# Conditioning products in column groups between the halves of the input projection, one stream of half-size weight units, gate rows by way of DRAM

## The reference

```python
mod = jnp.einsum('bd,de->be', jax.nn.silu(cvec), p['ada_w'][l]) + p['ada_b'][l]
sh1, sc1, g1, sh2, sc2, g2 = [m[:, None, :] for m in jnp.split(mod, 6, axis=-1)]
h = _rmsnorm(x, p['norm1_w'][l]) * (1 + sc1) + sh1
mix, s_fin = _mixer(h, rows, s0, l, p)      # input projection, 4 HGRN2 heads | Hyena long conv, output projection
x = x + g1 * mix
h = _rmsnorm(x, p['norm2_w'][l]) * (1 + sc2) + sh2
x = x + g2 * _convffn(h, rows, l, p)
```

## Time and profile before

| | |
|---|---|
| median of 3 runs | 1003.29 us (1003.22 to 1003.38) |
| span of the profiled execution, first to last instruction | 1001.4 us |
| PE busy | 979.4 us, 98% |
| DVE busy | 644.8 us, 64% |
| ACT busy | 346.6 us, 35% |
| DMA | 97.01 MB, mean 97 GB/s |

### The profile page before, as it was taken

How to read it: one execution, slowest core, us unless ns; L and a number is a source line. 1 busy time by engine, 2 the same in 40 slices (tenths; PEclk the granted TensorE clock), 3 DMA queues, 4 the chain that set the end, 5 groups by cost and what they waited for, 6 DMA issues and landing times.

```text
span 1001.4 us, 13700 instructions
## 1 busy us (share of the span) xinstructions
PE 979.4 (98%) x5628; PEld 835.9 (83%) x5628; DVE 644.8 (64%) x815; ACT 346.6 (35%) x590; POOL 0.2 (0%) x4
## 2 busy tenths in 40 slices
PE   7999999999999999999999999999999999999996
PEld 1257899999999994288849999988999988899985
DVE  4883458787786976947367656644566654466665
ACT  2552543444435313042164343311333331133333
POOL 0000000000000000000000000000000000000000
PEclk9999999999999999999999999999999999999999
DMA  7815332111211112824251212222122221121102
GB/s 288 329 72 173 122 126 85 49 43 44 80 52 44 48 48 98 294 81 154 99 210 43 85 47 80 85 84 85 43 85 84 84 85 68 59 85 63 45 20 105
DMA packets 17559, 97.01 MB, mean 97 GB/s; under 512 B 1912, under 2 KB 4472, under 8 KB 7257
## 3 DMA queue, kind: packets, MB, share of 16 engines
q1 hardware_dynamic: 17496, 96.14, 26.8%
HBM read 92.98 MB, written 3.15 MB: 96 GB/s over the span
## 4 chain that ended last, share of the span: by engine, by line
PE 93%; DVE 3%; ACT 2%; issue 1%; DMA 0%; SPq 0%; ACTq 0%; DVEq 0%
PE ps L1159 24%; PE ps L1161 24%; PE ps L1160 24%; PE ps L1178 7%; PE ps L1365 3%; PE ps L1484 1%; PE ps L1267 1%; PE ps L1377 1%; PE ps L1205 1%; PE ps L1297 1%; PE ps L1457 1%; PE ps L1258 1%; PE ps L1472 0%; PE ps L1385 0%; PE ps L1354 0%
## 5 line engine op out<-in xcount | busy, mean ns | idle before, releaser
L1159 PE MATMUL ps<-h_hi,w_hi 128*128 128x320 f32 x1152 | 360.8, 313 | 0.6 <-DVE h_lo L779 0.6
L1161 PE MATMUL ps<-h_hi,w_lo 128*128 128x320 f32 x1152 | 356.5, 309 | 0.0
L1160 PE MATMUL ps<-h_lo,w_hi 128*128 128x320 f32 x1152 | 356.3, 309 | 0.0
L771 DVE TENSOR_TENSOR w_lo<-raw,w_hi 128x1024 fp32r<-128x1024 f32 x114 | 138.8, 1225 | 140.8 <-ACT w_hi L487 135.9
L1159 PEld LDWEIGHTS ps<-h_hi,w_hi 128*128 128x128 f32 x1152 | 216.5, 188 | 1.6 <-DVE h_lo L779 0.9
L1160 PEld LDWEIGHTS ps<-h_lo,w_hi 128*128 128x128 f32 x1152 | 216.5, 188 | 0.3
L1161 PEld LDWEIGHTS ps<-h_hi,w_lo 128*128 128x128 f32 x1152 | 216.3, 188 | 0.0
L487 ACT ACTIVATE w_hi<-raw 128x1024 fp32r<-128x1024 f32 x114 | 118.7, 1051 | 134.4 <-PE ps L1161 128.1
L1159 PE MATMUL ps<-w_hi,a_hi 128*128 128x512 f32 x220 | 86.9, 395 | 0.0
L1160 PE MATMUL ps<-w_lo,a_hi 128*128 128x512 f32 x220 | 86.9, 395 | 0.0
L1161 PE MATMUL ps<-w_hi,a_lo 128*128 128x512 f32 x220 | 86.9, 395 | 0.0
(11 more groups left out here) (252 smaller groups left out, 1081.2 us busy)
## 6 DMA issues: line engine op xcount, KB each, us to landing
raw<-in_slots SPq DMA_DIRECT2D x76, 1024.0 KB, 4.8
xin<-in_x_sample SPq DMA_DIRECT2D x4, 512.0 KB, 6.9
x<-in_x_sample SPq DMA_DIRECT2D x4, 512.0 KB, 5.6
out_y_sample<-x SPq DMA_DIRECT2D x4, 512.0 KB, 2.6
decay<-in_decay SPq DMA_DIRECT2D x1, 1280.0 KB, 12.1
ktab<-in_ktab SPq DMA_DIRECT2D x1, 1024.0 KB, 6.8
utab<-in_utab SPq DMA_DIRECT2D x1, 1024.0 KB, 4.8
itab<-in_itab SPq DMA_DIRECT2D x1, 1024.0 KB, 4.9
```

The costliest lines, as they stand in the source:

```text
L771: V.tensor_tensor(w_lo[:, n % SPLITS, :], raw[:, s % RAWS, u * UNIT:(u + 1) * UNIT], w_hi[:, n % SPLITS, :].bitcast(F32), ALU.subtract).th ...
L1159: mm(out, lhs[0], rhs[0], start=first, stop=False)
L1160: mm(out, lhs[0], rhs[1], start=False, stop=False)
L1161: return mm(out, lhs[1], rhs[0], start=False, stop=last)
```

## The change

The 12 conditioning blocks are now all made alike: a quad (`ada_quad`) is four float32 products, each of one 128-row part of the sum, with a stationary side of 32 columns (silu(c) padded with zeros) and outputs on PSUM partitions 0, 32, 64 and 96, that is in four column groups. Two quads make a block. ACT copies all 128 partitions out, `ada_turn` transposes four 128 x 128 pieces, and DVE adds up the four groups (`sum_groups`). Blocks 0 to 3 stay at the start. The other eight stand in the input projection, at half products 7, 8 | 12, 13 | 19, 20 | 24, 25 | 31, 32 | 36, 37 | 43, 44 | 48, 49 (`ADA_QUAD`), with the turn behind the half product after (`ADA_TURN`: 9, 14, 21, ...). The blocks in stages 3 and 5, the fine units, and the gate products are gone: POOL writes the gate columns to a DRAM tensor `gates` and loads them back to all partitions. The stream of weights goes in units of 512 KB through a ring of five, with four split units and a lead of three. Half products use three PSUM banks where they used four; POOL issues the loads of masks, states, tables and x1 that SyncE issued. Within a head's tiles the last two (`g` and `hy`) are swapped, and the buffers `gs` and `cv` are single.

```diff
-RAWS = 3
-SPLITS = 3
+RING = 5
+SPLITS = 4
+def ada_half(e):
+    i = e - ADA_EARLY
+    return 7 + 12 * (i // 2) + 5 * (i % 2)
+ADA_QUAD = {ada_half(e) + j: (e, j) for e in range(ADA_EARLY, len(ADA_ORDER)) for j in range(2)}
+ADA_TURN = {ada_half(e) + 2: e for e in range(ADA_EARLY, len(ADA_ORDER))}
+ADA_SUM = {ada_half(e) + 3: e for e in range(ADA_EARLY, len(ADA_ORDER))}
+LEAD = 3
...
-            return n % 4 if n < NH else 5 + (n - NH) % 3
+            return n % 3 if n < NH else 5 + (n - NH) % 3
...
# POOL
+            def gate_out(which):
+                eng.wait_ge(sem("mod_ready"), ADA_ORDER.index(5 + 6 * which) + 1)
+                col = (2 + 3 * which) * KD
+                for s in range(2):
+                    eng.dma_start(gates[which, s].rearrange("(k p) -> p k", p=P), mod[:, col:col + KD, s],
+                                  allow_slow_non_contiguous=True).then_inc(sem("gate_out"), 16)
...
+            load(grow[:, :, :, :], gates.partition_broadcast(P), "ld_gates")
...
# ACT, loop over half products
                     spread(src, padm[:, i % 2, :], half, "half_free")
+                if n in ADA_TURN:
+                    ada_row(ADA_TURN[n])
                 if step_at(n):
                     step(*step_at(n))
...
-            for b in range(4, 8):
-                ada_row(b)
...
# PE
+            def ada_quad(e, j):
+                bank = ADA_BANK[e]
+                if j == 0 and e >= ADA_EARLY:
+                    eng.wait_ge(sem("ada_taken"), e)
+                elif j == 0 and bank in ADA_BANK[:e]:
+                    eng.wait_ge(sem("ada_row"), e - ADA_BANK[:e][::-1].index(bank))
+                for g in range(GROUPS):
+                    piece = arrived(eng, ("ada", e, 2 * j + g // 2))
+                    last = mm(ps[g * GROUP:(g + 1) * GROUP, bank, :], silu_c[:, GROUPS * j + g, :],
+                              piece[:, g % 2 * HW:(g % 2 + 1) * HW], start=(j == 0), stop=(j == 1))
+                last.then_inc(sem("ada_used"), 1)
+            def ada_turn(e):
+                eng.wait_ge(sem("ada_row"), e + 1)
+                if e:
+                    eng.wait_ge(sem("ada_taken"), e)
                 for k in range(4):
+                    last = nc.tensor.transpose(ps[:, TURN_BANK, k * P:(k + 1) * P],
+                                               ada_buffer(e)[:, k * P:(k + 1) * P], ident[:, :])
                 last.then_inc(sem("ada_cols"), 1)
...
-                half_product(n, tile_unit(n // 2), n % 2)
-                if n % 2 and n // 2 < MIXED - IV:
-                    fine_unit(IV + n // 2)
+                half_product(n, UNIT_TILE + n // 2, n % 2)
+                if n in ADA_QUAD:
+                    ada_quad(*ADA_QUAD[n])
+                if n in ADA_TURN:
+                    ada_turn(ADA_TURN[n])
                 if step_at(n):
                     step(*step_at(n))
...
-            eng.wait_ge(sem("uspec_ready"), 4)
-            ada_blocks(4, 8)
             eng.wait_ge(sem("zspec_ready"), 3)
...
-            ada_blocks(8, 10)
...
-            turn(xn, 1, (), gate_between)
-            eng.wait_ge(sem("row_ready"), 8)
+            turn(xn, 1, (), lambda k: None)
```

More of the change, by code:

```diff
@@ L101 @@
 ADA_SLOTS = [*range(ADA1), *range(SLOT_ADA2, SLOT_WOUT), *range(SLOT_ADA3, SLOT_FFN)]
-SLOT_UNITS = [RAW] * SLOT_FFN
+FFN_UNITS = []
+_s = SLOT_FFN
 for _f0, _nf in ROUNDS:
[L104 to L116, removed]
@@ L119, with weight_source @@
-UNIT_WOUT = MIXED + IV + len(TILES)
-UNIT_FFN = UNIT_WOUT + 2 * WOUT
+    _counts = [RAW] * _nf + 2 * [min(4, _nf - f) // 2 for f in range(0, _nf, 4)]
+    for _n in _counts:
+        FFN_UNITS += [(_s, _u) for _u in range(_n)]
+        _s += 1
+NSLOT = _s
+UNIT_TILE = IV
+UNIT_WOUT = IV + len(TILES)
+UNIT_FFN = UNIT_WOUT + 2 * WOUT
+NU = UNIT_FFN + len(FFN_UNITS)
+def weight_source(n):
+    if n < IV:
+        return SLOT_IV + n, 0
+    if n < UNIT_WOUT:
+        t = n - UNIT_TILE
+        at = t - (MIXED - IV)
+        return (SLOT_IV + IV + t, 0) if at < 0 else (SLOT_IV + MIXED + at // 2, at % 2)
+    if n < UNIT_FFN:
+        return SLOT_WOUT + (n - UNIT_WOUT) // 2, (n - UNIT_WOUT) % 2
+    return FFN_UNITS[n - UNIT_FFN]
@@ new lines, with stream @@
+ADA_SUM = {ada_half(e) + 3: e for e in range(ADA_EARLY, len(ADA_ORDER))}
+LEAD = 3
+def stream():
+    out = [("ada", e, q) for e in range(ADA_EARLY) for q in range(PIECES)]
+    out += [("weight", n) for n in range(UNIT_TILE + LEAD)]
+    for t in range(len(TILES)):
+        if t + LEAD < len(TILES):
+            out.append(("weight", UNIT_TILE + t + LEAD))
+        for n in (2 * t, 2 * t + 1):
+            if n in ADA_QUAD:
+                e, j = ADA_QUAD[n]
+                out += [("ada", e, 2 * j), ("ada", e, 2 * j + 1)]
+    return out + [("weight", n) for n in range(UNIT_WOUT, NU)]
@@ L579, in _ @@
                 take_odd(n)
-            for n in range(2, 2 * IV + 1):
+            for n in range(2, UNIT_TILE + LEAD):
                 split_hi(n)
@@ L617, in _ @@
                 src = ps[:, half_bank(n), 0:HT]
[L618 to L622 removed]
+                for unit in ahead(n):
+                    split_hi(unit)
                 eng.wait_ge(sem("half_made"), n + 1)
```

382 lines of the change are left out of this document (152 added, 230 removed).

## The result

The changed kernel takes 1029.43 us, median of 4 runs (1025.82 to 1030.04), against 1003.34 before: 1.0246 times as long, 95% interval 1.0227 to 1.0265. A second measurement on another chip gave 1.0238 (1.0221 to 1.0254). The forecast was 1035.7 us within 1014 to 1058, slower with 0.90. Direction and size came out. The profiled execution took 1025.82 us with a span of 1024.0. The terms are another matter: the quad was priced at more than twice what it costs, and two terms that cost more than forecast, the start and the gate products with norm2, made up for part of that. That the total came within 6.3 us is luck in part.

A forecast was written before the change was run, and what follows sets the result against it. TensorE was taken to bound the input projection, DVE to make the Hyena stage's hole. Terms 42.6 - 1.6 - 3.6 - 5.0 = +32.4 us on the 1001.4 span, 1033.8; with 1.9 for the median 1035.7 us, range 1014 to 1058.

The forecast's parts named there:

- start: Blocks 0 to 3 cost less TensorE time, but the second turn waits for a DVE sum: 0, bounds -3 and +3.
- input projection: Sixteen quads 36.0, turns 3.6, waits 10.4, fine units -7.4: +42.6 us, in the stage where TensorE sets the time.
- Hyena stage, to the output projection: Inverse transform can start 3.8 us earlier, less 2.2 charged for TensorE's start from idle: -1.6 us, bounds -3.8 and 0.
- gate products and norm2: Gate records in the output projection go, -3.6 us; norm2's first modulation comes earlier, less half the idle charge, -5.0 us.
- ConvFFN: Same products, and weight units of half the size arrive far ahead of use: 0 us.
- The mechanism: Conditioning moves out of two holes into the input projection, where TensorE has none; slower by over 0.2% given 0.90.
- The hidden work's end: Hyena stage: TensorE's four conditioning blocks fill a hole DVE makes anyway; only 3.8 us stick out and come back.
- Price of a quad: Input projection: eight passes of four matmuls take five pass times, 2.25 us a quad; bounds 0.87 and 3.5 us.
- rival 1: Input projection: the four column groups overlap fully, a quad takes 0.87 us; about +8 in all, 1012 us; chance 0.13.
- Turns and their waits: Input projection, eight times: four transposes at 0.45 us, and 1.3 us of TensorE waiting for ACT's copy; 3.6 and 10.4 us.
- Clock: Hyena stage: after idling 25.7 us TensorE's first products run slower, 2.2 us charged; half of it again at norm2.

The follow-up runs named there:

- e2: Changed kernel with blocks 6, 7, 10 and 11 run as quads in the Hyena stage, where PE waits for DVE's spectra: 1016.64 us, 1.0103.
- e6: Changed kernel with all four products of a quad written to the same 32 rows instead of four column groups: 1069.14 us, 1.0645.
- the second profile: The changed kernel itself measured once more, unedited, on another chip: 1028.42 us, 1.0238 of the kernel before.
- e4: Changed kernel with DVE's first two conditioning sums earlier and ScalarE's first two weight splits later, at the start only: 1026.65 us, 1.0216.
- e3: Changed kernel with the five x1 loads issued by SyncE inside the weight stream instead of by GpSimd: 1019.51 us, 1.016.
- e11: Changed kernel with later turns, four blocks in the Hyena stage, x1 on SyncE, reordered start, and unused products there and in the start's gaps: 1000.71 us, 0.9963.
- e9: Changed kernel with 30 unused products filling PE's empty stretch in the Hyena stage almost to its end: 1024.08 us, 1.0203.
- e7: Changed kernel with turns a half product later, four blocks in the Hyena stage, x1 on SyncE and the reordered start together: 1001.74 us, 0.9976.

## Why the prediction was right, step by step

The table's differences between before and after, against the sum on record:

| term | forecast | measured |
|---|---|---|
| start | 0 | +5.9 |
| input projection | +42.6 | +22.7 |
| Hyena stage, to the output projection | -1.6 | -1.3 |
| gate products and norm2 | -3.6 - 5.0 | -1.6 |
| ConvFFN | 0 | -3.1 |
| span | +32.4 | +22.6 |

Each length is from one profile of either kernel; how far a stage repeats is said above.

*The mechanism* held: conditioning moved out of two holes into the stage that PE sets, the holes stayed, and the time rose. The hidden work's end was right to 0.1 us: 3.8 forecast to come back in the Hyena stage, 49.89 - 46.13 = 3.76 measured. e2 shows the same from the other side: four blocks put back cost nothing there.

*Price of a quad: the mis-sized term.* The prediction took 2.25 us from "the order does not allow full overlap"; it is 1.0, near its lower bound of 0.87. Four matmuls of two passes each do run side by side in four column groups; e6 shows that without the groups they take 3.6. The step that failed is the sentence that only the second pass of one can lie beside the first of the next: the windows above show four passes that start together and four more 0.45 us later. By the prediction's own sign ("Wrong, if a quad takes 0.9 or 3.5 us") this term was wrong. The price was rival 1's, to which I gave 0.13. Sixteen quads: 16 us for 36.0. The factor between 3.62 and 1.00 us, 3.6, agrees with the up to 4x of the Trainium skill (TensorEngine Tiling (Array Packing), Theoretical Speedup) and not with the reading of program order that I set against it.

*Turns and their waits.* 0.45 each was right; the wait was 1.05, not 1.3. With 16 + 3.6 + 8.4 - 7.4 = 20.6 some 2 us of the stage's 22.7 are left, part of it the step behind a quad, whose rows are 1.28 and 1.38 us long.

*Start: forecast 0, bounds 3 either way; 5.9 measured, and 8.8 in the second profile.* The wait that I named (the second turn, for a sum behind the fourth filter tile) is there at 6.5 us in the changed kernel, and ACT waits 3.2 us for a raw unit with the first modulation queued behind it; I had not followed ACT's queue. e4 gets back about 3. (In e3 this wait is 8.5 us and the V product still starts at 74.46, so its length alone is not what it costs.) A second part was not foreseen at all: the filter taps. Before and in the changed kernel:

```profile
23.25 3.70 PE L1205 MATMUL ps<-w,hid 64*128 64x512 f32 x8
```

```profile
22.22 10.61 PE L1234 MATMUL ps<-w,hid 64*128 64x512 f32 x12 [1.45 <-ACT hid L596]
```

0.46 us and 0.88 us a record: PE runs at half pace until past 32 us. In the one profile whose V product starts at 74.46 (e3) the taps have the quick pace again, eight in 3.70 us. So of the 5.9 us some 4.6 go with the slow taps and 1.3 are there without them. That the shorter quads cause it by leaving PE emptier is argued. For it: the taps are quick in both profiles with long products among them, of the kernel before and of e6 (eight in 3.70 us from 22.94 on), and slow in eleven of the twelve with quads of 1.0 us. Against it: e3 is the twelfth, and in e11, filled with small products, they stay slow.

*Gate products and norm2: forecast -8.6, measured -1.6.* The bound was named ("If x1, now issued by POOL, came late, that gain would go") and the wrong end of it chosen: x_prompt lands 11.7 us after its issue, and PE waits 5.4. With the loads back on SyncE (e3) the stage is 83.81 - 75.93 = 7.9 us shorter than before, so the 8.6 was nearly right as a price of what was removed. Of the 7.9, 5.7 lie behind the output projection's last product, for 5.0 forecast, and 2.2 ahead of it, for 3.6.

*Clock.* 2.2 us charged in the Hyena stage. Found: 2.5 on the first 16 records (6.20 for 3.72) and 2.3 by e9, and 1.6 to 3.0 from inverse to output over the eight profiles that leave PE empty ahead of it.

*ConvFFN:* forecast 0, measured -3.1, cause open.

So errors of -19.9 (projection), +5.9, +0.3, +7.0 and -3.1 leave -9.8 us on the span. The largest, one term at more than twice its size, is covered by two that the prediction put too low: the direction was earned by the mechanism, the closeness of the total is luck. The median lay 3.6 us above the profiled execution, which brings it to 6.3 below the forecast. Rival 1 had the right price and the total 1012, 17 us too low: its other terms were mine.

## What to carry to other kernels

Work that fills a hole costs its sticking-out end, not its length; moved into the stage that sets the time it costs its length, its hand-overs and the small waits it makes. When a change moves work, list what every queue holds behind each new wait, also on the engines whose work did not change: ACT's two splits and five loads on another queue (waits of 3.2 and 5.4 us) cost about as much here as the eight waits that I had counted (8.4). And where two bounds lie a factor of four apart, one product measured alone is worth more than an argument about order.

## What the runs showed of the hardware that I had not expected

- Four float32 products of 32 weight columns and 512 moving columns, two passes each, in four column groups: 1.0 us together, four passes starting within 0.03 us and the other four 0.45 us later; one behind the other in one group 3.62.
- PE left empty for 5.6 us before the inverse transform paid as much as when it stood 26.2 us (6.57 and 6.20 us for the 16 records); at 0.5 us it paid nothing (3.72), as at 2.1 us in e2 (3.72), while at 2.6 us in e7 it paid (5.41).
- Between 25 and 35 us the granted clock reads 1.00 in the changed kernel while its products take 0.88 us, the pace of half speed. In e3, where the column falls to 0.50 at 15 to 20 us and rises again, they take 0.46. There the durations are to be believed, not the column.
- The pace of the filter taps' products sorts the starts: the V product at 74.5, 79.1 to 79.5 or 81.9 to 82.5 us in kernels with the same start.
